# Gathering the expert layers' token rows once, into packed slots, and copying each pair's slots from there

## What is computed

```python
# per token, for its two experts e with weights w_e (block 1: D_FF 256, block 2: 512)
y = sum(w_e * ((silu(x @ w_gate[e]) * (x @ w_up[e])) @ w_down[e]))
# block 1 adds a shared expert (256 wide) that every token uses
```

## Time and profile before

| | |
|---|---|
| median of 3 executions | 1110.01 us (1107.6 to 1110.35) |
| the profiled execution: span, first to last instruction | 1109.3 us |
| PE, matmuls busy | 1021.5 us (92%) |
| DVE / ACT / GpSimd busy | 338.6 / 155.8 / 35.7 us |
| moved by DMA | 340.13 MB, mean 307 GB/s |
| mean granted TensorE clock | 0.977 of 2.4 GHz |

### The profile page before, as it was taken

The page is one execution under the profiler, slowest core; times in us unless marked ns, Lnnn a source line. Parts: engine busy times, 40 slices in busy tenths (PEclk is TensorE's granted clock), DMA queues, the critical chain, the costliest instruction groups (busy, mean ns, idle before and its releaser), DMA issues.

```text
span 1109.3 us, 12940 instructions
## 1 busy us (share of the span) xinstructions
PE 1021.5 (92%) x4993; PEld 594.4 (54%) x4993; DVE 338.6 (31%) x691; ACT 155.8 (14%) x357; POOL 35.7 (3%) x67
## 2 busy tenths in 40 slices
PE   6998969999999999979999599999998989898985
PEld 4676537676766676566654535353535344343532
DVE  2344144334334334330420522222131222221213
ACT  3232132000001000121341200000000000000002
POOL 3000220000000000000001100000000000000000
PEclk9999988999999999989999799999999999999998
DMA  9930332588998888944333189999999999999994
GB/s 322 343 120 1 121 126 77 194 357 365 415 373 364 365 361 366 392 175 169 120 134 109 47 347 421 420 422 422 421 422 422 422 422 421 422 423 421 422 421 179
DMA packets 61124, 340.13 MB, mean 307 GB/s; under 512 B 10300, under 2 KB 11344, under 8 KB 23840
## 3 DMA queue, kind: packets, MB, share of 16 engines
q1 hardware_dynamic: 55536, 337.60, 75.7%
q10 hardware_dynamic: 5136, 1.87, 0.7%
q0 software_dynamic: 416, 0.16, 0.1%
HBM read 338.56 MB, written 1.05 MB: 306 GB/s over the span
## 4 chain that ended last, share of the span: by engine, by line
PE 78%; DMA 13%; DVE 5%; ACT 2%; issue 1%; SPq 0%; DVEq 0%; ACTq 0%
PE ps L707 25%; DMA ring<-in_expert_w_up_dram 13%; PE ps L739 12%; PE ps L693 11%; PE ps L1543 7%; PE ps L1685 4%; PE ps L755 4%; PE ps L1756 4%; PE ps L1720 1%; PE ps L1533 1%; PE ps L1658 1%; PE ps L719 1%; PE ps L1626 1%; ACT xs L964 1%; PE ps L925 1%
## 5 line engine op out<-in xcount | busy, mean ns | idle before, releaser
L707 PE MATMUL ps<-ring,work 128*64 128x256 f32 (+1 forms) x2048 | 341.7, 489 | 26.0 <-DMA ring<-in_expert_w_up_dram 16.2
L707 PEld LDWEIGHTS ps<-ring,work 128*64 128x64 f32 x2048 | 149.2, 138 | 219.7 <-issue 173.6
L739 PE MATMUL ps<-ring,work 128*64 128x512 f32 x768 | 172.1, 596 | 0.8 <-ACT work L532 0.7
L693 PEld LDWEIGHTS ps<-parts 128*128 128x128 f32 x512 | 125.7, 336 | 11.1 <-issue 10.4
L693 PE MATMUL ps<-parts 128*128 128x256 f32 x512 | 128.7, 407 | 1.6 <-DVE parts L577 1.6
L739 PEld LDWEIGHTS ps<-ring,work 128*64 128x64 f32 x768 | 52.4, 137 | 97.8 <-issue 96.6
L606 DVE TENSOR_TENSOR work<-work,ps 128x256 f32<-128x256 f32 (+1 forms) x32 | 17.8, 555 | 269.6 <-PE ps L707 269.6
L1543 PE MATMUL ps<-xT,ring 128*128 128x256 f32 (+1 forms) x384 | 88.6, 389 | 1.3 <-issue 1.3
L1543 PEld LDWEIGHTS ps<-xT,ring 128*128 128x128 f32 x384 | 73.6, 194 | 14.3 <-issue 2.2
L755 PE MATMUL ps<-parts 128*128 128x512 f32 x256 | 74.3, 412 | 1.6 <-DVE parts L627 1.6
L597 DVE TENSOR_TENSOR work<-ps,gk 128x512 f32<-128x512 f32 x64 | 44.3, 692 | 96.2 <-PE ps L693 96.2
(11 more groups left out here) (301 smaller groups left out, 613.0 us busy)
## 6 DMA issues: line engine op xcount, KB each, us to landing
ring<-in_expert_w_gate_dram SPq DMA_DIRECT2D x64, 1024.0 KB, 19.2
ring<-in_expert_w_up_dram SPq DMA_DIRECT2D x64, 1024.0 KB, 22.6
ring<-in_expert_w_down_dram SPq DMA_DIRECT2D x64, 1024.0 KB, 16.8
ring<-in_w_gate_dram SPq DMA_DIRECT2D x32, 1024.0 KB, 8.1
ring<-in_w_up_dram SPq DMA_DIRECT2D x32, 1024.0 KB, 9.8
ring<-in_w_down_dram SPq DMA_DIRECT2D x32, 1024.0 KB, 6.8
ring<-in_w_in_dram SPq DMA_DIRECT2D x18, 1024.0 KB, 13.5
ring<-in_w_out_dram SPq DMA_DIRECT2D x8, 1024.0 KB, 10.9
```

Source lines behind the costliest of these rows:

```text
L693: mm = pe.matmul(ps[:, 6 + b, c * 2 * P:(c + 1) * 2 * P], v[:, tt, feature::KC].bitcast(F32R), onehot[:, tt, :].bitcast(F32R), start=(k + ...
L707: mm = pe.matmul(ps[CAP * e:CAP * e + CAP, 4 + which, 0:ff], xgT[:, k0 + k, P * odd + CAP * e:P * odd + CAP * e + CAP], chunks[e][:, k, :] ...
L739: mm = pe.matmul(ps[CAP * e:CAP * e + CAP, 6 + half, :], hT[:, c0 + k, CAP * e:CAP * e + CAP], chunks[e][:, k, 512 * half:512 * half + 512 ...
```

## The change

- A layer gathers once. DVE scans the experts' counts into `first_slot`, so that the 512 assignments stand packed by expert in `SLOTS` = 512 columns. Each token's two slots are found with two `max` instructions (`top8`), and `onehot` is built over 512 columns, per token tile by a compare and a compare-and-add. PE then makes 8 x 4 matmuls of 512 columns, one feature block per bank, through banks 4 to 7; DVE takes the even blocks and ACT the odd ones to `xgP` (8 x (512 + 64) columns), times the gain. All the later gathers and their `onehot`s fall away.
- For each pair, ACT copies two windows of 8 x 64 columns out of `xgP` into `xg2` (two buffers). The start of a window is read from `starts_i` in SBUF into a register, and the copy's source address is made with it. The copy for pair n+1 stands at the head of ACT's work for pair n. The first pair's first expert is read from `xgP` directly, and its second one is copied in two halves.
- Block one: DVE's weights of the experts (`weigh_experts`, cut off from `route`) and the bias, distance and lambda work, and ACT's `decay` exponentials, move ahead of the shared expert's silu and product. In block two `weigh_experts` moves behind DVE's takes of the gathered rows.
- DVE's loop does one pair per turn instead of two. GpSimd makes a table 1..512 at the program's start and DVE casts it. Buffers are laid out anew.

```diff
@@ moe_scalar
+            def take_gathered(f):
+                act.wait_ge(ev("gathered"), KC * turn + f + 1)
+                act.activation(xgP[:, f, 0:SLOTS], ps[:, 4 + f % 4, :], ACT.Copy, scale=gk[:, cfg["gains"], f:f + 1])\
+                    .then_inc(ev("xgP_odd"), 1)
+            def window(e):
+                return bass.ds(act.value_load(starts_i[0:1, bass.ds(e, 1)], min_val=0, max_val=SLOTS), CAP)
+            def bring(pair, buf, done):
+                for e in range(2):
+                    act.activation(xg2[:, buf, :, CAP * e:CAP * e + CAP], xgP[:, :, window(2 * pair + e)], ACT.Copy)\
+                        .then_inc(done, 1)
+            def pair(n, m, sfx="", bring_next=None):
+                if bring_next is not None:
+                    bring(*bring_next, ev("xg"))
                 act.wait_ge(*products_done(cfg, m, gates, sfx))
                 act.activation(sil[:, 0:ff], ps[:, 4, 0:ff], ACT.Silu).then_inc(ev(f"sil{sfx}"), 1)
...
+            take_gathered(1)
+            take_gathered(3)
+            act.wait_ge(ev("placed"), 5 * TURN[tag])
+            second = window(1)
+            for half in range(2):
+                act.wait_ge(ev("xgP_even"), 4 * turn + 2 * half + 2)
+                act.wait_ge(ev("xgP_odd"), 4 * turn + 2 * half + 2)
+                act.activation(xg2[:, 0, 4 * half:4 * half + 4, CAP:2 * CAP], xgP[:, 4 * half:4 * half + 4, second],
+                               ACT.Copy).then_inc(ev("xg"), 1)
+                if half == 0:
+                    take_gathered(5)
+                    take_gathered(7)
@@ moe_vector
+            for f in range(0, KC, 2):
+                take_gathered(f)
+            if tag == "m2":
+                weigh_experts(dve, tag, chain)
             count_rounds(dve, tag, chain)
-            take_gathered(EARLIER[tag] // 2)
@@ moe_tensor
+            def gather():
+                for f in range(KC):
+                    if f == 0:
+                        pe.wait_ge(ev("onehot"), TT * TURN[tag])
+                    if f == 3:
+                        pe.wait_ge(ev("placed"), 5 * TURN[tag])
+                    if f >= 4:
+                        pe.wait_ge(ev("xgP_odd" if f % 2 else "xgP_even"), 4 * turn_ + (f - 4) // 2 + 1)
+                    for k, v in enumerate((xs_high, xs_low)):
+                        for tt in range(TT):
+                            mm = pe.matmul(ps[:, 4 + f % 4, :], v[:, tt, f::KC].bitcast(F32R),
+                                           onehot[:, tt, :].bitcast(F32R), start=(k + tt == 0), stop=(k + tt == 2))
+                    mm.then_inc(ev("gathered"), 1)
...
+                if not first:
+                    pe.wait_ge(ev(f"xg{sfx}"), n * 2 + 2)
...
+                        if first and which == 0 and k0 % 4 == 0:
+                            pe.wait_ge(ev("xg"), n * 2 + (2 if k0 + rows_ > 4 else 1))
+                            pe.wait_ge(ev("xgP_even"), 4 * turn_ + 3)
...
-                    if ahead:
-                        gather(g + 1, 0, free=q * 2 + EARLIER[tag])
                     if not first_pair:
                         scatter(done, 0, opens, False)
-                    if ahead:
-                        gather(g + 1, 1)
-
-                        pe.wait_ge(ev("xg"), g * 4 + 7)
                     turn_hidden(n)
@@ place
+            chain(dve.tensor_tensor_scan(first_slot[:, 1:EXPERTS + 1], ones[:, 0:EXPERTS], ps[:, 7, 192:224], 0.0,
+                                         ALU.mult, ALU.add))
+            first = first_slot[:, 0:EXPERTS].unsqueeze(1).broadcast_to([P, TT, EXPERTS])
+            chain(dve.scalar_tensor_tensor(slot_of, pos, 1.0, first, ALU.add, ALU.add))
+            chain(dve.tensor_tensor(slot_of, slot_of, routed, ALU.mult))
+            for tt in range(TT):
+                chain(dve.max(top8[:, tt, :], slot_of[:, tt, :]))
+            for tt in range(TT):
+                chain(dve.tensor_scalar(onehot[:, tt, :].bitcast(F32R), from_one[:, :], top8[:, tt, 0:1], None,
+                                        ALU.is_equal))
+                dve.scalar_tensor_tensor(onehot[:, tt, :].bitcast(F32R), from_one[:, :], top8[:, tt, 1:2],
+                                         onehot[:, tt, :], ALU.is_equal, ALU.add).then_inc(ev("onehot"), 1)
...
+            dve.tensor_copy(starts_i[:, :], first_slot[:, 0:EXPERTS]).then_inc(ev("placed"), 1)
+            dve.memset(xgP[:, :, SLOTS:SLOTS + CAP], 0.0).then_inc(ev("placed"), 1)
```

More of the change, by code:

```diff
@@ L50 @@
 CAP = 64
+SLOTS = 2 * TOK
 PAIRS = EXPERTS // 2
@@ L293, in two_block_kernel @@
         e_t = m(TT, EXPERTS)
-        lg = m(TT, 36)
-        assert 2048 + 512 * 3 + 1024 + 256 + 7 * 64 + 72 <= 5632
-        lgT = m(TOK, start=17664 - TOK)
+        slot_of = m(TT, EXPERTS)
+        bias = m(DH, TOK)
+        decay = m(DH, TOK)
+        dist = m(TOK)
+        assert 4608 + 2048 + 1536 + 1024 + 256 + 8 * 64 + 2048 + 256 <= UNDER
+        lg = m(TT, 36, start=KC * (SLOTS + CAP))
+        lgT = m(TOK)
+        dist_i = y[:, 0:TOK].bitcast(I32)
         exact = carve(parts)
-        y_high = exact(D)
+        xs_high = exact(TT, D)
+        xs_low = exact(TT, D)
+        onehot = exact(TT, SLOTS)
+        y_high = exact(D, start=0)
         y_low = exact(D)
         scat = exact(TT, P)
[L301 to L304, removed]
+        assert UNDER + parts.shape[1] <= 17664
+        spare = (xT[:, :, :].rearrange("p c t -> p (c t)")[:, 0:CH], work[:, 14592:14592 + CH])
         b = carve(work)
[L307 to L314, removed]
+        qdT = b(DH, TOK, start=5120)
         kdT = b(DH, TOK)
@@ L627, in take_y, with one_pair @@
                     dve.tensor_tensor(low.bitcast(F32R), v, high, ALU.subtract).then_inc(ev(f"y_parts{sfx}"), 1)
[L629 to L642, removed]
-            count_rounds(dve, tag, chain)
-            take_gathered(EARLIER[tag] // 2)
[L645 to L648, removed]
+            def one_pair(p, n):
+                build_weighted(p, n)
+                hidden(n, p)
+                take_scatter(n)
+                take_y(n)
+            for f in range(0, KC, 2):
+                take_gathered(f)
+            if tag == "m2":
+                weigh_experts(dve, tag, chain)
+            count_rounds(dve, tag, chain)
+            one_pair(0, EARLIER[tag])
+            with dve.Fori(1, PAIRS) as p:
+                one_pair(p, p + EARLIER[tag])
             dve.wait_ge(ev("rounds"), TURN[tag])
@@ L675, in moe_tensor, with gates_and_ups @@
             rows_ = CH // ff
[L677 to L700, removed]
+            turn_ = TURN[tag] - 1
+            def gather():
[11 more added lines that the diff above has]
+                    mm.then_inc(ev("gathered"), 1)
+            def gates_and_ups(get, used, n, odd, first=False, sfx=""):
+                if not first:
+                    pe.wait_ge(ev(f"xg{sfx}"), n * 2 + 2)
                 j = 0
@@ L758, in scatter, with two_pairs @@
                 return mm
-            def two_pairs(q, q_first, turn, first, last):
+            def two_pairs(q, q_first, turn, first):
                 def getter(odd):
@@ L773, in getter @@
                     return get
-                g = q + EARLIER[tag] // 2
                 for odd in range(2):
                     n = q * 2 + (EARLIER[tag] + odd)
-                    first_pair, ahead = first and not odd, odd and not last
+                    first_pair = first and not odd
                     if not first_pair:
@@ L1138, in _ @@
             route_scalar(act, "m1")
+            act.wait_ge(ev("lag_ready"), 1)
+            for hh in range(DH):
+                act.activation(decay[:, hh, :], dist, ACT.Exp, scale=LN_GAMMA[hh]).then_inc(ev("decay_raw"), 1)
+            act.wait_ge(ev("lam_a"), 1)
+            act.activation(lam_b, lam_a, ACT.Exp).then_inc(ev("lam_b"), 1)
             for tt in range(TT):
```

159 lines of the change are left out of this document (76 added, 83 removed).

## The result

The changed kernel takes 1073.78 us (median of 4; 1070.63 to 1079.12), the one before 1110.13 (median of 4, with one execution more than the 1110.01 above). The ratio is 0.9684, with a 95% interval of 0.9662 to 0.9705: **3.2% faster**, 36 us. The forecast was 1073.5.

A forecast was written before the change was run, and what follows sets the result against it. The prediction took m1 to be bound by PE and m2 by its loads. 1109.3 - 40.5 (m1) + 3.8 (m2's start) = 1072.6, with 0.7 of the median over the span 1073.3, stated as 1073.5; range 1066 to 1084.

The forecast's parts named there:

- The shift of the bound: m1's pairs: loads take over from PE, 14.9 us a pair against 13.0; m1 ends at start + 224.6.
- m1's start: Before m1's first gate product: gather stays 8.1 us, take and copy behind it add about 0.5; start 205.3.
- the strided load: m1's gather: the strided weight load, not the columns, sets the 0.25 us pace of a matmul.
- the lost cover: m1's start: moved work fills DVE's idle time, costed at nothing; without that cover 6 us would go onto the start.
- ACT per pair: Two register reads (0 to 0.6 us each) and two copies (1.4 at most) per pair, hidden beside gates and ups: nothing.
- Block two's mixer: Between m1 and m2: the ring arrives empty instead of full, yet this costs nothing.
- the empty ring: Block two's mixer: 12 us pass before its first product and chunks are used slower than one per 2.48 us; nothing.
- m2's start: From counts to m2's first gates: onehot +2.0, gather partly at low clock +2.6, wait for the take -0.8; +3.8 us.
- m2's pairs: m2: seven gathers, 53 us, leave PE, but nothing comes of it since the loads set the pace.
- Rival B: PE's clock falls after waits at loads in m1's and m2's pairs, making the kernel slower, 1143 us; chance 3%.

The follow-up runs named there:

- Experiment 1: Every expert chunk's load halved from each layer's third pair on, in both kernels: kernel before 1080.12 us (0.9736), changed kernel 977.31 us (0.8809).
- experiment 5: Changed kernel with the gather's weights read as 128 neighbouring elements instead of every eighth: 1072.54 us in one run.
- experiment 4: Changed kernel with block one's moved bias, distance, lambda and decay work and the shared expert's silu put back in their old order: 1073.97 us (0.9686).
- experiment 2: Changed kernel with extra ACT copies of 2048 elements at the head of each pair: two copies 1075.59 us (0.9703), four copies 1108.16 us (0.9989).
- after_light: Changed kernel with only the first half of every expert chunk loaded from each layer's third pair on: 977.31 us (0.8809).
- Experiment 6: Changed kernel with products of constants on PE where it waits ahead of both layers and block two's mixer: 1081.29 us; with about half as many 1064.49 us.
- experiment 3: Changed kernel with eight more reads of a start from SBUF into a register per pair on ACT: 1072.53 us (0.9662).

## Why the prediction was right

**The shift of the bound.** m1 was to end 224.6 us after its first gate product, and took 224.4. In it two errors cancel. The first load is issued 3.9 us after the first product, not 5.6, since the clock did not fall there; and the last ups were used at 414.80, 211.4 us after the start, where 1.7 less for that reason would have given 210.2. The lag of data behind the issue and of PE behind the data was thus 1.2 us more than I took. That the end fits within 0.2 us is luck; the bound itself is not. Experiment 1 shows the mechanism: PE alone would take 210.7 us (predicted 211) and the loads keep the rest.

**m1's start.** Predicted 205.3, measured 203.4 and 204.7. The two parts that I priced cost more than the +0.5 that I took: from the gather's start to the first gate product it is 10.0 us for 8.9 in both profiles. The wait for take and copy is +0.8 for +0.5, and the gather of 512 columns took 8.4 us for 8.1; I had left it at 8.1, with 11.4 as the bound. What lies ahead of the gather, and moves between profiles, covered this. 8.4 is near 8.1, so weights do load beside 512 columns. Whether the strided load set the pace of the 256 columns, as I said, isn't shown; of the 8.4 us experiment 5 takes 0.5. The price of the lost cover, +6, was wrong: experiment 4 finds 1 us, since most of the moved work runs while PE gathers.

**ACT per pair** at nothing: right, with the reads at 0.53 us where 0 to 0.6 was allowed, and 3.6 us more of ACT work (two copies of experiment 2) still free.

**Block two's mixer** at nothing: not refuted, though the first profile looks so. From m1's end to the last output product 141.5 us went by in it, for 139.4; in the second profile it was 139.6. No wait at a load shows there, so the empty ring costs nothing. The difference is the clock. Timelines of the mixer's first four blocks, in the first and the second profile of the changed kernel, and busy time by stretch in the first:

```profile
440.77 29.73 PE L1571 MATMUL ps<-xT,ring 128*128 128x256 f32 x128 [1.28 <-issue]
```

```profile
441.96 27.86 PE L1571 MATMUL ps<-xT,ring 128*128 128x256 f32 x128 [1.28 <-issue]
```

```profile
435.00:440.00 5.00, 3.65 (x16) 3.28 (x16) 3.50 (x6) 1.78 (x5) 0.00 (x0) 0.50 1.05 386
440.00:444.00 4.00, 3.23 (x8) 2.63 (x9) 0.00 (x0) 0.67 (x3) 0.00 (x0) 0.50 1.04 394
```

PE stood 8 us between m1's last scatter and the transposes, and its clock was at half from before 435 to about 444, with the first products of the mixer in it (29.7 us for 27.9 in the first four blocks). The second profile has the same pause, and its clock was back at 1.00 when those products began, as in the kernel before, where they began at 483.1:

```profile
478.00:483.00 5.00, 3.39 (x16) 3.23 (x16) 3.09 (x6) 2.04 (x7) 0.00 (x0) 0.66 0.81 296
483.00:486.00 3.00, 2.90 (x14) 2.60 (x15) 0.00 (x0) 0.00 (x0) 0.00 (x0) 1.00 0.02 7
```

Of the eight profiles with this mixer unchanged (the two, and those of `after_light` and of experiments 2 to 5), five have 29.7 to 30.0 us there and three 27.9. The two of the kernel before have 27.9. So the 2.1 us aren't shown to be an effect of the change; what sets the moment at which the clock rises stays open. Experiment 6 fills the pause, and its 138.7 us are under all of these.

**m2's start.** Predicted +3.8, measured +3.3. `onehot` came 2.2 us later (2.0 predicted). The gather at the low clock took 9.9 us, not 10.6, as the clock rose some 4 us after its start (0.50 up to 594, 0.82 from there to 596), not 6.3; that term was +2.6 less 0.8 and is +1.1 in all. The second profile has the same 9.9 and +3.3.

**m2's pairs** at nothing although 53 us of PE's work left them: 470.9 us for 471.9. With half the loads 54 us arrive.

**The sum.** Against the kernel before, in the forecast, the first and the second profile:

| | forecast | first | second |
|---|---|---|---|
| start of m1 | +0.5 | -1.4 | -0.1 |
| m1 | -40.9 | -41.1 | -41.2 |
| mixer | 0 | +2.1 | +0.2 |
| m2's start | +3.8 | +3.3 | +3.3 |
| m2 and the norm | 0 | -1.0 | -1.2 |
| span | 1072.6 | 1071.2 | 1070.3 |

The shift in m1 and the step at m2's start are what the change does; the lines of m1's start and of the mixer differ by 1.3 and 1.9 us between two profiles of one kernel. That the forecast of 1073.5 lies 0.3 us from the measured median is in part luck: the spans were 1.4 and 2.3 us shorter than forecast, and the median lies 2.6 us over the first of them, not 0.7.

The Trainium skill, "DMA: Bandwidth & Descriptors", Specifications, lists an HBM limit of about 358 GB/s per core; by an estimate from that figure m1 would have stayed at its old pace. The trace does not agree, with 422 GB/s through m1. The same page says, under "Measured", that each core gets about 358 when both cores of the HBM domain stream; here one core ran, so the figure was no bound for this kernel.

Rival B's falls of the clock did not come in the changed kernel's pairs: waits of up to 1.4 us, clock 1.00. They did come in experiment 2 with four copies, in ten of fourteen pairs, behind stops of 1.8 us.

## What to carry to other kernels

When work is taken off the engine that sets the pace, ask which bound stands next, and give it the new length: here 54 us of PE's work in each of two layers were worth 41 in the one that PE bound and 1 in the one that the loads bound. A buffer that runs ahead delays the new bound (eight of sixteen pairs still ran at PE's pace), so the layer's time is that of the whole stream from its first freed slot, not of the steady beat. And where a stretch begins with a stop of PE, look at the granted clock of what follows: at m2's start the gather of 512 columns took 9.9 us, against 8.4 at full clock in m1, while the one of 256 columns had taken 8.0, no more than its 8.1 in m1. And take a second profile before a stretch's microseconds are given a cause: 2 us of the mixer came and went between two profiles of one kernel.

## What the runs showed of the hardware

- One core's loads ran at 420 to 422 GB/s for 200 us in m1 (214 to 414 us) and at 422 for 444 us in m2 (606 to 1050), beside a PE that was busy 95% and 84% of that time.
- A read of a word of SBUF into a register of ACT costs about 0.53 us when nothing hides it (experiment 3).
- Stops of PE of 1.3 to 1.4 us, one in each 14.9 us of m1, left the clock at 1.00; with stops of 1.8 us in each pair the pair was longer by 1.6 us in ten of fourteen, with a granted clock of 0.68 in the stretch read. A stop's length alone does not tell: at m1's start a clock of 0.50 followed one of 0.78 us in the kernel before, and 1.00 one of 1.59 us after the change. Constant products, 9 of 0.87 us around the counts, held it at 1.00 through m2's start.
- A float32 product of 128x128 weights with 512 columns takes 0.87 us at full clock, nearly four times the 0.23 of the scatter's float32r products take.
